# Six input norms of a two-layer transformer kernel, applied behind the products instead of ahead of the transposes

## The reference

```python
def rmsnorm(x, g):
    y = xf * lax.rsqrt(jnp.mean(xf * xf, axis=-1, keepdims=True) + NORM_EPS)
    return (y * g.astype(jnp.float32)).astype(x.dtype)

def second_block(x, norm_gains, ...):
    for layer in range(2):
        g = norm_gains[layer]
        h = rmsnorm(x, g[0])
        x = x + 0.5 * rmsnorm(swiglu(h, gate0, up0, down0), g[1])
        h = rmsnorm(x, g[2])
        x = x + rmsnorm(token_mixer(h, w_in, w_out, ...), g[3])
        h = rmsnorm(x, g[4])
        x = x + 0.5 * rmsnorm(swiglu(h, gate1, up1, down1), g[5])

def swiglu(h, w_gate, w_up, w_down):
    return (jax.nn.silu(h @ w_gate) * (h @ w_up)) @ w_down
```

## Time and profile before

| what | us |
|---|---|
| median of 3 runs | 1531.22 (1525.55 to 1538.05) |
| the profiled execution | 1529.79 |
| its span, first to last instruction | 1528.0 |
| TensorE busy | 1471.6 (96%) |
| VectorE busy | 966.6 (63%) |
| ScalarE busy | 704.6 (46%) |
| second block, from the first joint's first idle matmul at 481.47 | 1046.5 |

### The profile page before, as it was taken

The page is one execution under the profiler, slowest core; times in us unless marked ns, Lnnn a source line. Parts: engine busy times, 40 slices in busy tenths (PEclk is TensorE's granted clock), DMA queues, the critical chain, the costliest instruction groups (busy, mean ns, idle before and its releaser), DMA issues.

```text
span 1528.0 us, 21855 instructions
## 1 busy us (share of the span) xinstructions
PE 1471.6 (96%) x8075; PEld 1179.7 (77%) x8075; DVE 966.6 (63%) x1529; ACT 704.6 (46%) x1207; POOL 67.6 (4%) x97
## 2 busy tenths in 40 slices
PE   5899999989999999999999999999999999999998
PEld 3778746877854888878887888878888789688887
DVE  1588425246334677777777777686766875867775
ACT  2533236141244454456565444364443656554443
POOL 0200220020001000000010000000000000100000
PEclk9899999989999999999999999999999999999999
DMA  9622156235315556546424655446564643345552
GB/s 312 202 83 83 55 173 231 83 118 175 111 55 176 188 183 208 202 154 166 139 90 143 207 193 197 156 151 227 170 211 145 205 142 139 103 161 196 197 198 73
DMA packets 197908, 244.52 MB, mean 160 GB/s; under 512 B 4400, under 2 KB 178896, under 8 KB 197712
## 3 DMA queue, kind: packets, MB, share of 16 engines
q1 hardware_dynamic: 194272, 229.43, 45.9%
q0 software_dynamic: 2992, 12.06, 2.3%
q10 hardware_dynamic: 576, 2.10, 0.4%
HBM read 242.52 MB, written 1.05 MB: 159 GB/s over the span
## 4 chain that ended last, share of the span: by engine, by line
PE 84%; DVE 6%; ACT 3%; DMA 3%; issue 2%; POOL 0%; SPq 0%; DVEq 0%; ACTq 0%
PE bank L1650 35%; PE bank L2092 19%; PE bank L2093 10%; PE bank L1739 5%; PE bank L2014 2%; DMA weight_ring<-in_w_ada 2%; DVE weights_low L1303 2%; PE bank L1628 1%; DMA weight_ring<-in_w_ffn_gate 1%; PE bank L1959 1%; ACT weights_high L845 1%; PE bank L1922 1%; PE bank L1671 1%; PE bank L1881 1%; PE bank L2060 1%
## 5 line engine op out<-in xcount | busy, mean ns | idle before, releaser
L2092 PE MATMUL bank<-input_split,weights_high 128*128 128x512 f32 x1408 | 501.9, 399 | 1.7 <-DVE input_split L1342 1.3
L1303 DVE TENSOR_TENSOR weights_low<-weight_ring,weights_high 128x1024 fp32r<-128x1024 f32 x328 | 396.3, 1223 | 150.3 <-ACT weights_high L845 148.4
L845 ACT ACTIVATE weights_high<-weight_ring 128x1024 fp32r<-128x1024 f32 x328 | 338.3, 1053 | 193.8 <-PE bank L2093 56.7
L2093 PE MATMUL bank<-input_split,weights_low 128*128 128x256 f32 x1408 | 395.2, 281 | 0.0
L2092 PEld LDWEIGHTS bank<-input_split,weights_high 128*128 128x128 f32 x1408 | 264.5, 188 | 69.5 <-issue 2.2
L2093 PEld LDWEIGHTS bank<-input_split,weights_low 128*128 128x128 f32 x1408 | 265.9, 189 | 3.0
L1650 PE MATMUL bank<-weights_high,hidden_high 128*128 128x512 f32 x352 | 138.6, 394 | 1.8 <-DVE hidden_low L1388 1.6
L1650 PE MATMUL bank<-weights_low,hidden_high 128*128 128x512 f32 x352 | 137.9, 392 | 0.0
L1650 PE MATMUL bank<-weights_high,hidden_low 128*128 128x512 f32 x352 | 137.1, 389 | 0.0
L910 ACT ACTIVATE hidden_high<-hidden 128x256 fp32r<-128x256 f32 x88 | 36.8, 418 | 186.2 <-DVE hidden L1384 179.5
L1650 PE MATMUL bank<-input_split,weights_high 128*128 128x256 f32 x512 | 94.7, 286 | 1.4 <-ACT qk_feature_major L965 0.6
(11 more groups left out here) (317 smaller groups left out, 2059.2 us busy)
## 6 DMA issues: line engine op xcount, KB each, us to landing
weight_ring<-in_w_ffn_gate SPq DMA_DIRECT2D x44, 1024.0 KB, 6.1
weight_ring<-in_w_ffn_up SPq DMA_DIRECT2D x44, 1024.0 KB, 5.5
weight_ring<-in_w_ffn_down SPq DMA_DIRECT2D x44, 1024.0 KB, 4.9
weight_ring<-in_w_in SPq DMA_DIRECT2D x32, 1024.0 KB, 5.4
weight_ring<-in_w_ada SPq DMA_DIRECT2D x24, 1024.0 KB, 6.8
weight_ring<-in_w_out SPq DMA_DIRECT2D x16, 1024.0 KB, 4.9
weight_ring<-in_w_in SPq DMA_DIRECT2D x24, 512.0 KB, 5.1
gain_row<-in_norm_gains POOLq DMA_DIRECT2D x6, 512.0 KB, 3.9
```

The lines of the kernel that those rows point to most:

```text
L845: A(unit_in(WH, U), unit_source(U), ACT.Copy).then_inc(s_high, 1)
L1303: TTn(unit_in(WL, U), unit_source(U), unit_in(WH, U).bitcast(F32), ALU.subtract).then_inc(s_low, 1)
L2092: mm(b[:, :].rearrange("p (h n) -> p h n", h=2), unit_in(WH, U)[:, k, :], HX[:, k, :, :], start=(k == 0), stop=False, skip_group_check=True)
L2093: last = mm(b[:, 0:T], unit_in(WL, U)[:, k, :], HH[:, k, :], start=False, stop=(k == KD - 1), skip_group_check=True)
```

## The change

The rows are transposed unscaled. A norm's inverse root is a factor per token, so it can be applied behind the product.

- **Joint.** TensorE transposes `X` itself as soon as the residual's halves are there, first tile 0, then tile 1, into banks 4, 5, 2, 3, 6, 7, 6, 7 (`X_BANK`). One idle matmul stands ahead of the transposes (12 at the first joint) and one behind tile 0's first four. All eight chunks are copied and subtracted one by one, with the gain as a scale. The gain rows that POOL fetched for columns 512 to 1023 are gone, as are VectorE's scaling passes and its squares. Of the residual's squares ScalarE makes tile 0's ahead of the copies and tile 1's behind them and behind `high` 3 (`x_mean`).
- **The factor.** VectorE takes the reciprocal of both roots and writes it to a diagonal (`norm_diag`), TensorE multiplies that by ones (`norm_sum`, behind two units of the site) so that each of 128 partitions has the factor of every token in a row, and ScalarE copies the row to SBUF (`norm_row`) between `high` 4 and `high` 5.
- **FFN.** `gate_sum` multiplies the sum by `norm_row` ahead of Silu: one more VectorE instruction of 128x256 a chunk, with a wait on its own sum. The up half isn't scaled. Its factor is the same for a token's whole output, so it falls out of the output norm, whose constant is multiplied by the mean square (`eps_scaled`). The Silu table is loaded in the joint.
- **Mixer.** All q and k blocks are evicted by VectorE, times `norm_row`; v blocks times the factor per token. The first two blocks use banks 0 and 1.
- **The closing norm of the first block** works in halves instead of whole rows.

The core of the diff (comment lines name the engine):

```diff
-WARM = 4
+WARM = 12
+X_BANK = (4, 5, 2, 3, 6, 7, 6, 7)
...
-    PB2.setdefault((kind, blocks[0]), 6 + len(PB2) % 2)
+    PB2.setdefault((kind, blocks[0]), len(PB2) if len(PB2) < 2 else 6 + len(PB2) % 2)
...
+        norm_row, norm_diag = ytmp[:, 0, 0:T], ytmp[:, 1, 0:T]
...
 # ScalarE
+            def x_mean(i, t):
+                for hf in range(2):
+                    act.wait_ge(*(at("x_new", i - 1, t, hf) if i else at("final_scaled", t, hf)))
                     A(unread, X[:, t, hf * 512:(hf + 1) * 512], ACT.Square, accum_out=stat[:, 2 * t + hf:2 * t + hf + 1]).then_inc(*done("sum_squares", "site", i, t, hf))
...
+                A(stat[:, 6 + t:7 + t], stat[:, 2 * t + 1:2 * t + 2], ACT.Identity, bias=stat[:, 4 + t:5 + t], scale=1.0 / D).then_inc(*done("x_mean", i, t))
 
             def site_norm(i):
+                x_mean(i, 0)
+                for c in range(KD):
+                    act.wait_ge(*at("x_T", "site", i, c if c < 4 else 4 + c % 2))
+                    if c >= 6:
+                        act.wait_ge(*at("input_ready", i, c - 2))
+                    half = c // 6
+                    A(HH[:, c, :], B[X_BANK[c]][:, half * T:(half + 1) * T], ACT.Copy, scale=vT[:, 2, R_PRE + 8 * i + c:R_PRE + 8 * i + c + 1]).then_inc(*done("input_high", i, c))
+                high(unit_base[i] + 3)
+                x_mean(i, 1)
...
+                A(stat[:, 8:10], stat[:, 6:8], ACT.Sqrt).then_inc(*done("rms_ready", "site", i))
+                if SITES[i][0] == "ffn":
+                    A(stat[:, 60:61], eps[:, 0:1], ACT.Silu)
+                high(unit_base[i] + 4)
+                act.wait_ge(*at("norm_sum", i))
+                A(norm_row, B[4][:, 0:T], ACT.Copy).then_inc(*done("norm_row", i))
+                high(unit_base[i] + 5)
...
 # ScalarE, projected() of mix
-                        b = blocks[0]
-                        if kind == "qk" and b % 2 == 0:
-                            act.wait_ge(s_used, u0 + unit + 1)
-                            A(FQ[:, b, :], B[PB2["qk", b]][:, 0:T], ACT.Copy, scale=QKSC[b]).then_inc(*done("qk_ready_act", n, b))
...
 # VectorE
             def site_norm(i):
...
-                    TS(XN2[:, t, cut], X[:, t, cut], stat[:, 12 + t:13 + t], None, ALU.mult).then_inc(*done("x_scaled", "site", i, t, 0))
...
+                for c in range(KD):
+                    half = c // 6
+                    dve.wait_ge(*at("input_high", i, c))
+                    STT(HL[:, c, :], B[X_BANK[c]][:, half * T:(half + 1) * T], vT[:, 2, R_PRE + 8 * i + c:R_PRE + 8 * i + c + 1], HH[:, c, :].bitcast(F32), ALU.mult, ALU.subtract).then_inc(*done("input_ready", i, c))
+                low(unit_base[i] + 3)
+                dve.wait_ge(*at("rms_ready", "site", i))
+                dve.reciprocal(stat[:, 12:14], stat[:, 8:10]).then_inc(*done("inverse", "rms", "site", i))
...
+                    last = TS(norm_diag[:, t * P:(t + 1) * P], ident, stat[:, 12 + t:13 + t], None, ALU.mult)
+                last.then_inc(*done("norm_diag", i))
...
+                for unit in range(4, SPLIT):
+                    low(unit_base[i] + unit)
...
-                    if t == 0 and i < 5:
-                        dve.wait_ge(*at("x_new", i, 0, 0))
-                        dve.tensor_tensor_reduce(out=XN2[:, 0, 0:512], in0=X[:, 0, 0:512], in1=X[:, 0, 0:512], ...
...
-                def gate_sum(par, used, j=None):
+                def gate_sum(par, used, ready, j=None):
                     dve.wait_ge(s_used, step(used, j, 6))
+                    dve.reduce_sum(gsum[:, par, :], B[2 * par][:, :].rearrange("p (h n) -> p n h", h=2), AXX).then_inc(s_added, 1)
+                    dve.wait_ge(s_added, ready)
+                    TTn(gsum[:, par, :], gsum[:, par, :], norm_row, ALU.mult).then_inc(s_gate, 1)
...
-                            last = CP(dst[:, t], src[:, t])
+                            last = TS(dst[:, t], src[:, t], stat[:, 12 + t:13 + t], None, ALU.mult)
-                    elif b % 2:
+                    else:
-                        TS(FQ[:, b, :], B[PB2["qk", b]][:, 0:T], QKSC[b], None, ALU.mult).then_inc(*done("qk_ready_dve", n, b))
+                        STT(FQ[:, b, :], B[PB2["qk", b]][:, 0:T], QKSC[b], norm_row, ALU.mult, ALU.mult).then_inc(*done("qk_ready", n, b))
...
 # TensorE
             def site_norm(i):
+                def turned(t, chunks):
+                    for c in chunks:
...
+                        pe.wait_ge(*(at("x_new", i - 1, t, c // 4) if i else at("final_scaled", t, c // 4)))
+                        last = tr(B[X_BANK[c]][:, half * T + t * P:half * T + (t + 1) * P], X[:, t, c * P:(c + 1) * P], ident)
...
+                warm(1 if i else WARM)
+                turned(0, (0, 1, 2, 3))
+                warm(1)
+                turned(0, (4, 5, 6, 7))
+                turned(1, (0, 1, 2, 3, 4, 6, 5, 7))
+
+            def norm_sum(i):
...
+                pe.wait_ge(*at("norm_diag", i))
                 for t in range(2):
+                    last = mm(B[4][:, t * P:(t + 1) * P], ones, norm_diag[:, t * P:(t + 1) * P], start=True, stop=True)
+                last.then_inc(*done("norm_sum", i))
...
                 gate_up(0, a, f0 if n else None, None, i)
+                norm_sum(i)
...
-                products(0, 4)
+                products(0, 2)
+                norm_sum(i)
+                products(2, 4)
```

More of the change, by code:

```diff
@@ L623, in _ @@
                     nxt = i + 1
-                    pool.wait_ge(*at("x_scaled", "site", i, 1, 1))
-                    load(pre_row[:, 512:D], I["norm_gains_2"][nxt // 3, 2 * (nxt % 3), 512:D].partition_broadcast(P), "pre_loaded")
                     pool.wait_ge(*at("y_gained", i, 1, 1))
@@ L1035, in _ @@
                 site_norm(i)
-                for unit in range(EARLY, SPLIT):
-                    high(unit_base[i] + unit)
                 if i == 1:
@@ L1311, in _ @@
                 dve.wait_ge(*at("inverse", "final", t))
[L1312 removed]
+                for hf in range(2):
+                    cut = slice(hf * 512, (hf + 1) * 512)
+                    STT(X[:, t, cut], X[:, t, cut], stat[:, 12 + t:13 + t], gain_row[:, cut], ALU.mult, ALU.mult).then_inc(*done("final_scaled", t, hf))
             def lambdas():
@@ L1390, in ffn @@
                 a = unit_base[i]
-                gate_sum(0, a + 1)
+                dve.wait_ge(*at("norm_row", i))
+                gate_sum(0, a + 1, f0 + 1)
                 product(0, a + 2, f0 + 1)
                 hidden_low(0, f0 + 1)
-                gate_sum(1, a + 3)
+                gate_sum(1, a + 3, f0 + 2)
                 low(a + 6)
@@ L1405, in pair @@
                     split = [U for U in range(a + 6, a + 12) if U < last_pair + 5]
-                    gate_sum(0, a + 1, j)
+                    gate_sum(0, a + 1, step(f + 1, j, 2), j)
                     for U in split[0:1]:
@@ L1412, in pair @@
                         low(U, j)
-                    gate_sum(1, a + 4, j)
+                    gate_sum(1, a + 4, step(f + 2, j, 2), j)
                     for U in split[3:4]:
@@ L1428, in ffn @@
                 low(a + 5)
-                gate_sum(1, a + 3)
+                gate_sum(1, a + 3, f + 2)
                 low(a + 6)
@@ L1591, in _ @@
                 site_norm(i)
-                for unit in range(EARLY, SPLIT):
-                    low(unit_base[i] + unit)
                 if i == 1:
@@ L2056, in site_norm, with warm @@
             def site_norm(i):
+                def warm(count):
+                    for _ in range(count):
+                        mm(B[0][:, :], ident, KB[:, 0:512], start=True, stop=True)
+                def turned(t, chunks):
+                    for c in chunks:
+                        half = c // 6
+                        if t == 0 and half == 0:
+                            for r in hand_over(X_BANK[c], ("input_ready", i, c if c < 4 else c + 2)):
+                                pe.wait_ge(*at(*r))
+                        pe.wait_ge(*(at("x_new", i - 1, t, c // 4) if i else at("final_scaled", t, c // 4)))
+                        last = tr(B[X_BANK[c]][:, half * T + t * P:half * T + (t + 1) * P], X[:, t, c * P:(c + 1) * P], ident)
+                        if t and (c < 4 or half):
+                            last.then_inc(*done("x_T", "site", i, c if c < 4 else c - 2))
@@ L2057, in site_norm @@
                 for r in hand_over(0):
                     pe.wait_ge(*at(*r))
-                for _ in range(WARM if i else 3 * WARM):
-                    mm(B[0][:, :], ident, KB[:, 0:512], start=True, stop=True)
-                for t in range(2):
-                    for c in (0, 2, 1, 3, 4, 5, 6, 7):
-                        pe.wait_ge(*at("x_scaled", "site", i, t, c // 4))
-                        bank, half = (4 + c % 2, c // 2) if c < 4 else (c // 2, c % 2)
-                        if t == 0 and half == 0:
-                            for r in hand_over(bank, ("input_ready", i, c + 2 if c < 4 else c)):
```

(7 more changed lines are left out.)

78 lines of the change are left out of this document (26 added, 52 removed).

## The result

The changed kernel takes 1542.82 us in the median of 16 runs (1540.73 to 1546.15), the kernel before 1531.15 (16 runs, 1525.55 to 1538.05): ratio 1.0078, 95% interval 1.0066 to 1.0089, 11.7 us slower. The profiled execution took 1544.76, with a span of 1543.0, 15.0 more than that of before.

A forecast was written before the change was run, and what follows sets the result against it. TensorE's own work was 84% of the span, with weight supply level with it. FFNs +10.4, tails +1.3, mixers -2.0 and clock +3.0 gave +12.7 on 1529.8 (median 1531.2): 1543 us, range 1529 to 1551.

The forecast's parts named there:

- inner joint, first product after its start: At the five inner joints: first product 5.25 us after the joint's start instead of 7.71, 2.45 gained each.
- first joint, first product: First joint: twelve idle matmuls stay and one more follows; first product at 495.1 instead of 494.20, 0.9 lost.
- first down product, new wait: FFN opening: first down product waits until 18.8 though TensorE is ready at 17.7, 1.1 of new wait.
- gate issue after the first product: FFN opening: gate transfer issued 21 us after the first product, not 16.65; 2.05 later from the joint's start.
- wait before the third down product: Third down product in each FFN: TensorE waits 2.4, 2.8, 3.2 and 3.4 us for the late gate transfer.
- third down product, from the joint's start, FFN 1: First FFN: gate goes out at 516.3, so the third down product starts at 529.0 instead of 523.68, 5.3 lost.
- FFN 2, 3, 4: Third down product of the later FFNs: 1.4 lost in the second, 1.7 in the third, 2.0 in the last.
- three tails: Last pair of three FFNs: the added 0.43 goes straight through the serial work, +1.3 together.
- mixers, from joint to joint: Both mixers: joint gains less norm_sum and longer waits; 0.65 gained in the first, 1.35 in the second, together -2.0.
- clock: Behind the new waits at the third down product: half clock follows two of four, 1.5 of work each, +3.0.
- The supply had no room: Rival at the gate's landing: if ScalarE has it within 4.7 of issue, 1528 to 1530, no slower; chance 0.15.
- The joints didn't lose the clock: Rival at the joints: half clock follows transposes and short waits, about 1.5 each, up to +9, 1552; chance 0.15.

The follow-up runs named there:

- the wait filled: Changed kernel with three idle 512-column matmuls on TensorE before each FFN's third down product: 1539.87 us, 1.0073 of the kernel before.
- the chunk's work first: Changed kernel with the third chunk's sums, Silu and splits ahead of the splits of units 10 and 11 in each FFN's first pair: 1530.50 us, ratio 0.9997.
- the queues set to the new order of events: Changed kernel, third chunk's work first, first gate sum ahead of splits, 8 first-joint idle matmuls, one next-site unit ahead at tails: 1521.54 us, ratio 0.9953.
- the order together with the tail: Kernel before, with the third chunk's work first and the last chunk's hidden_high and hidden_low ahead of the next site's splits: 1532.10 us, ratio 1.0006.
- the gate sum first: Changed kernel with the first chunk's gate sum ahead of the splits of units 4 and 5, and norm_row copied before high 4: 1536.59 us, ratio 1.0049.
- the tail with none ahead: Changed kernel with the last chunk's hidden_high and hidden_low ahead of all splits of the next site's first units: 1545.21 us, ratio 1.0090.
- 8 idle matmuls: Changed kernel with 8 idle matmuls instead of 12 at the first joint: 1541.17 us, 1.0067 of the kernel before.
- no idle in the joints: Changed kernel without the two idle matmuls in each of the five inner joints, first joint unchanged: 1544.06 us, 1.0095 of the kernel before.

## Why the prediction was right, and where it was not

The time (1543 against 1542.8) and the direction held. Step by step, in the profiled executions:

| step | predicted | measured |
|---|---|---|
| inner joint, first product after its start | 5.25 | 5.24 to 5.31 |
| first joint, first product | +0.9 | +0.75 |
| first down product, new wait | 1.1 | 1.03 to 1.12 |
| gate issue after the first product | 21.15 | 21.10 to 21.12 |
| wait before the third down product | 2.4 to 3.4 | 2.34 to 2.96 |
| third down product, from the joint's start, FFN 1 | +5.3 | +4.97 |
| FFN 2, 3, 4 | +1.4, +1.7, +2.0 | +1.83, +2.12, +1.66 |
| three tails | +1.3 | +1.3 (0.82 each) |
| mixers, from joint to joint | -0.65, -1.35 | -0.38, -1.00 |
| clock | two spells of 1.5, +3.0 | four of 1.6 to 1.7, +6.6 |
| sum for the second block | +12.7 | +17.1 |

**The mechanism** held at every step up to the gate's issue, to a tenth. The joint gives 2.4 five times, 12 in all, and wherever an FFN follows, all of it is given back by the third down product: 1.1 in the wait before the first down product, 0.6 for `norm_sum` and the first unit's pace (13.73 - 1.12 against 12.02), the rest before the third.

**The clock** is the term that was mis-sized. All four waits tripped it and one spell costs 1.6 to 1.7 instead of 1.5: the fourth down product follows the third after 10.07 to 10.10, before after 8.38 to 8.48. The run with the wait filled shows that it is the idle time. I had one stretch as evidence and took the middle. The profiled second block came out 4.4 above the sum, the medians 1.0 below it (11.7 apart), so the hit on the microsecond is luck in part.

**The cause of the wait** was named wrongly. The prediction says that the weight supply is level with TensorE and that a transfer which VectorE releases is late. The transfer is late for ScalarE and VectorE, and TensorE waits because the third chunk's Silu and sum are queued behind its splits; with the chunk's work first, the same late transfer costs nothing at the third down product, where it had cost 2.3 to 3.0 and a spell, and the waits of 0.55 to 0.89 that are left further on are again work queued behind splits. The chain of waits shows the transfer and then, as "issue", ScalarE's split ahead of the Silu (1374.61 to 1375.45); I read the first and passed over the second. The arithmetic was the same either way, the repair is not.

**Mixers.** The waits are where they were put: 1.62 at the first scores of the first mixer, at 14.4 after its first product as worked out, and 0.19 in the second, where 0.2 was worked out; of the two that existed one shrank to 1.04 and the other grew to 1.35. The gain was 0.6 smaller than predicted. By the rows 0.25 in the first mixer and 0.4 in the second were lost before the first of these waits came; that wait, shorter than forecast, gave 0.2 back, and as much was lost behind it. Why stays open.

**The rivals.** The supply had no room: the gate was with ScalarE 7.5 to 8.1 after its issue, where 4.7 was the limit. From the last FFN's gate issue to its landing the stretch is (us, PE busy, granted clock, DMA share, GB/s):

```profile
1366.90:1374.38 7.48, 7.48 (x41) 1.00 0.97 338
```

So the rate is near the 358 GB/s that the Trainium skill gives (DMA: Bandwidth & Descriptors, Bandwidth), and 2.5 MB moved in that time. The estimate of 5.9 counted the down and the gate transfer; the up transfer, issued 1.0 after the gate, moved at the same time. The joints didn't lose the clock in the changed kernel; without their idle matmuls two of five did. The table load in the joint took 1.28, with ScalarE's instructions ending 0.02 ahead of it and starting 0.02 behind it, so the drain that the Trainium skill adds (ScalarE: Activation LUTs, What ACT_TABLE_LOAD costs) isn't seen here.

**The change itself** isn't at fault for the 12 us. With the queues set to the new order of events it is 7.7 ahead of the kernel before. That kernel gained nothing from the order together with the tail (1.0006); from the order alone it would have gained an estimated 1.1, so by that estimate the change is worth 6 to 7 us rather than 7.7. What made it slower stood around it: twelve idle matmuls sized for a chain that it removed, and splits ahead of work that now comes due first.

## What to carry to other kernels

When a stage ahead gets shorter or a step is added to a serial chain, go through each in-order queue behind it and ask which instruction has its inputs and stands behind one that hasn't; moving it cost nothing and was worth 14 of 17 us here, half clock included. A gap in a queue that waits for a buffer isn't free either: what filled it must go somewhere, and at the tail it went onto the path. In this kernel a new wait of TensorE of 1.9 to 3.4 us costs its length and nearly always 1.6 more for the clock, unless TensorE waits again soon behind it: then the slow work only shortens that wait.

## What the runs showed of the hardware

**Waits and the clock.** In the second blocks of seven executions with such waits (the changed kernel twice, the gate sum first, the tail with none ahead, 8 idle matmuls, no idle in the joints, before with order and tail), TensorE idled for 1.9 to 3.4 us 24 times, and 23 times the granted clock fell to 0.50 (1.2 of 2.4 GHz) between 1.0 ahead of the wait's end and 1.4 behind it. By (1 - granted clock) x length that is 1.7 each time and 3.4 once, a little less in work where it began inside the wait. The one exception was 2.28 long. Of 17 waits of 1.51 to 1.64 (third down products, joints, first scores, in ten executions) 3 were followed by it, of shorter ones none. The wait of 1.62 to 1.64 in the first mixer lost the clock in one execution and kept it in nine.

**Landing times.** The same gate transfer of 1 MB, issued between a down and an up transfer, had its first reader on ScalarE between 6.4 and 8.6 us after its issue in one FFN or another, with no pattern that I can name. In the two executions of the changed kernel the third down product started 4.5 behind that reader in all eight FFNs, so its waits of 2.2 to 3.2 vary as the landing does.

**The first block** took 476.7 to 487.8 us in executions of the same code, so a gain of five microseconds elsewhere doesn't show in a pair of single runs.
